# The scan's broadcast loads of the decay sums move from SyncE's queue to GpSimd's

## What is computed

```
a_cs    = cumsum(dt * a_neg)                      # decay sums, per token and head
decay   = exp(where(lower, a_cs[t] - a_cs[s], -inf))
y_diag  = einsum('tsh,shp->thp', cb * decay, xdt)  # cb = C B^T per group
y_off   = einsum('tn,hpn->thp', C, h_in) * exp(a_cs)
y       = y_diag + y_off + d_skip * x
state   = h_in * exp(a_cs[last]) + einsum('sn,shp->hpn', B, xdt * decay_end)
```

## Time and profile before

| | us |
|---|---|
| median of 3 runs | 1619.68 |
| lowest, highest | 1617.15, 1621.8 |
| profiled execution, its own time | 1623.28 |
| its span in the profile | 1621.5 |
| busy: PE, DVE, ACT, POOL | 1359.6, 830.5, 669.1, 265.7 |

### The profile page before, as it was taken

One profiled execution on the slowest core, in us unless ns is written; L12 is line 12 of the kernel. 1 busy time (PEld: TensorE's weight loads), 2 busy tenths in 40 slices (PEclk: granted clock), 3 DMA queues, 4 the chain that ended last, 5 costly groups with the idle time before them and its releaser, 6 DMA issues. The chain is left out here.

```text
span 1621.5 us, 20620 instructions
## 1 busy us (share of the span) xinstructions
PE 1359.6 (84%) x7925; PEld 1190.4 (73%) x7925; DVE 830.5 (51%) x953; ACT 669.1 (41%) x1028; POOL 265.7 (16%) x284
## 2 busy tenths in 40 slices
PE   3999989799998999668888826999974499999980
PEld 1789989799997889645656625998772388888860
DVE  2411432277663111026677666332536189999966
ACT  2423321144442222155567536111131277777753
POOL 0600000000000010044579750000005000000002
PEclk9899999999999999877899856999967699999995
DMA  9982121122112332343454341224246499999945
GB/s 387 405 321 78 53 78 53 36 78 79 60 71 94 128 122 80 115 158 114 132 164 163 130 182 69 79 100 156 93 162 238 158 371 397 415 414 412 404 176 207
DMA packets 61639, 289.09 MB, mean 178 GB/s; under 512 B 8171, under 2 KB 12787, under 8 KB 41206
## 3 DMA queue, kind: packets, MB, share of 16 engines
q1 hardware_dynamic: 48566, 242.18, 40.0%
q0 software_dynamic: 12608, 45.62, 7.2%
q10 hardware_dynamic: 384, 0.16, 0.0%
HBM read 239.51 MB, written 48.43 MB: 178 GB/s over the span
## 5 line engine op out<-in xcount | busy, mean ns | idle before, releaser
L212 PE MATMUL banks<-rounded,rounded 128*128 128x320 f32 (+1 forms) x1168 | 366.8, 314 | 20.1 <-DVE rounded L735 6.9
L213 PE MATMUL banks<-rounded,rounded 128*128 128x320 f32 (+1 forms) x1168 | 364.6, 312 | 0.0
L214 PE MATMUL banks<-rounded,rounded 128*128 128x320 f32 (+1 forms) x1168 | 364.5, 312 | 0.0
L212 PEld LDWEIGHTS banks<-rounded,rounded 128*128 128x128 f32 (+1 forms) x1168 | 221.7, 190 | 21.6 <-issue 13.9
L191 DVE TENSOR_TENSOR rounded<-words,rounded 128x2048 fp32r<-128x2048 f32 x52 | 119.2, 2292 | 226.3 <-ACT rounded L183 224.1
L1889 DVE TENSOR_TENSOR rounded<-words,rounded 128x2048 fp32r<-128x2048 f32 x93 | 212.9, 2290 | 32.9 <-ACT rounded L1880 32.1
L213 PEld LDWEIGHTS banks<-rounded,rounded 128*128 128x128 f32 (+1 forms) x1168 | 221.8, 190 | 0.4
L214 PEld LDWEIGHTS banks<-rounded,rounded 128*128 128x128 f32 (+1 forms) x1168 | 221.5, 190 | 0.3
L1880 ACT ACTIVATE rounded<-words 128x2048 fp32r<-128x2048 f32 x96 | 183.6, 1916 | 46.6 <-PE banks L2007 39.2
L183 ACT ACTIVATE rounded<-words 128x2048 fp32r<-128x2048 f32 x52 | 99.2, 1908 | 140.7 <-PE banks L233 62.7
L1185 ACT ACTIVATE words<-words,words 128x128 f32<-128x128 f32 x320 | 97.8, 388 | 75.4 <-DMA words<-decay_sums 75.4
(11 more groups left out here) (270 smaller groups left out, 2034.7 us busy)
## 6 DMA issues: line engine op xcount, KB each, us to landing
words<-in_units SPq DMA_DIRECT2D x52, 1024.0 KB, 4.9
words<-in_wg SPq DMA_DIRECT2D x32, 1024.0 KB, 8.1
words<-in_wu SPq DMA_DIRECT2D x32, 1024.0 KB, 8.6
words<-in_wd SPq DMA_DIRECT2D x32, 1024.0 KB, 9.4
words<-decay_sums SPq DMA_DIRECT2D x40, 512.0 KB, 3.7
words<-in_w_mod_rest SPq DMA_DIRECT2D x32, 512.0 KB, 5.0
slot_rows<-words POOLq DMA_DIRECT2D x27, 512.0 KB, 21.6
expert_rows<-words POOLq DMA_DIRECT2D x25, 512.0 KB, 9.6
```

Of the source, the lines that this page charges most:

```text
L212: nc.tensor.matmul(out, lhs[0](k), rhs[0](k), start=(k == 0), stop=False)
L213: nc.tensor.matmul(out, lhs[0](k), rhs[1](k), start=False, stop=False)
L214: last = nc.tensor.matmul(out, lhs[1](k), rhs[0](k), start=False, stop=(k == nk - 1))
```

## The change

POOL's program issues the 40 broadcast loads in place of SP's. The first four stand at the head of POOL's program, behind a wait for the stored sums. The others stand in POOL's loop: iteration j, from 1 to 36, issues the load of sub-step j + 3 behind `time_rows(j + 2)` and ahead of `weigh` and `finish_y(j - 1)`. The slots of `E`, the semaphore value that each load waits for and the one that it raises stay as they are. SP keeps the modulation pieces and the stores of the states.

```diff
         @block.sync
-            def spread(j):
-                c, g, q = subs[j]
-                n = (c * 2 * G + 2 * g + q) * 1024
-                if j >= SLOTS:
-                    sp.wait_ge(y_done, j - SLOTS + 1)
-                sp.dma_start(E[:, j % SLOTS, :], scr["sums"][:, n:n + 1024].partition_broadcast(P)).then_inc(sums_spread[j % SLOTS], 16)
...
-            sp.wait_ge(sums_stored, 16 * 16)
-            for j in range(SLOTS):
-                spread(j)
...
             for j in range(NS):
-                if j + SLOTS < NS:
-                    spread(j + SLOTS)
                 if j in at_sub:
                     store_piece(at_sub[j] - 1)
...
         @block.gpsimd
+            def spread(j):
+                c, g, q = subs[j]
+                n = (c * 2 * G + 2 * g + q) * 1024
+                if j >= SLOTS:
+                    pool.wait_ge(y_done, j - SLOTS + 1)
+                pool.dma_start(E[:, j % SLOTS, :], scr["sums"][:, n:n + 1024].partition_broadcast(P)).then_inc(sums_spread[j % SLOTS], 16)
+
+            pool.wait_ge(sums_stored, 16 * 16)
+            for j in range(SLOTS):
+                spread(j)
             pool.wait_ge(scales_done, 2)
...
                 if j + 2 < NS:
                     time_rows(j + 2)
+                if j and j + 3 < NS:
+                    spread(j + 3)
                 for x in x_at[j]:
                     weigh(pool, nc.gpsimd, x)
                 if j > N0:
                     finish_y(j - 1)
```

## The result

The changed kernel takes 1650.94 us (median of four runs, 1649.1 to 1658.53), the kernel before 1619.67 (1617.15 to 1621.8): 1.0203 of it, 95% interval 1.0167 to 1.0238. It is slower by 31.3 us; the forecast was 1620 with a range to 1628. The profiled execution has a span of 1649.9 us, 28.4 more than before. All of that lies in the scan: from the first L1273 to the last it was 220.6 us (710.95 to 931.59) and is 249.0 (710.60 to 959.60).

What follows compares the result with a forecast made beforehand. The scan was taken as bound by a loop of DVE's L1273, PE's products, state product and modulation row, with GpSimd filling up. Terms +0.7 - 1.6 - 0.8 + 1.1 + 0.5 = -0.1 us gave 1620 us, range 1613 to 1628.

Steps and rivals of the forecast that it cites:

- SyncE: 0, loads later: 0.: Removing 40 issues from SyncE gains 0; loads issued later in the scan still leave 2.5 us of room, cost 0.
- second rival: Scan loads from GpSimd land too late, so DVE waits for ACT at L1273: 1623.5 to 1625.5 us; slower-side chance 0.06.
- The price of an issue, 0.54: Each load issue on GpSimd takes 0.54 us, like its direct stores; 22 us more GpSimd work in all.
- first rival: Each GpSimd issue costs 1.29 us, like its indirect ones: about +7.4 us, 1627 us; chance 0.13.
- the third: Rival: DVE's products hold up the issue too, delaying weigh or finish_y: +3.2, 1623 us; counted within the likeliest 0.60.
- The start, +0.7: Four issues ahead of GpSimd's first weigh make it end at 692.9, and the first sub-step follows: +0.7 us.
- Step (b): Issue delays GpSimd's weigh, so L1273 goes first: -1.6 us at iterations 10, 22, 24; -0.8 at 4 and 6.
- (a): Issue hidden under a wait GpSimd has anyway, at iterations 12 to 20 (even), 25 to 29 and 31: 0.
- (d): Issue plainly in the way at iteration 30, where weigh ran alone and PE took it up at once: +0.5 us.
- Step (c): Issue pushes later GpSimd products into DVE's way at iterations 15, 17, 19, 21: +0.28 each, +1.1 us.
- fourth rival: GpSimd's and DVE's products fall in a favourable order, with fewer L1273 waits: -5.2 us, 1614.5 us; chance 0.08.
- The clock: Rival: shifted rhythm moves four PE sub-steps between clock levels, 6.7 us either way: 1613 (chance 0.07) or 1626 us (0.06).

## Why the prediction was wrong, by its own steps

*What bounds the kernel.* The loop that I named holds: DVE's product, PE's products, the state product, the modulation row. That GpSimd "fills up" led me to look for its delays there; it mattered as an obstacle in front of L1273, not as a full engine.

*SyncE: 0, loads later: 0.* Right. The late loads from SyncE cost nothing (0.9995), and the second rival is out: landing takes 4.2 us and at most 6.5, not the 8.8 and 10.3 of the earlier trace rows.

*The price of an issue, 0.54.* Right: 0.578 at the median, 0.597 at most. The first rival (1.29 us) is out, and so is the third, by which DVE's products hold up an issue: none of the 40 took over 0.597, and the one at 848.04 took 0.58 with L1273 running from 847.76 to 849.18.

*The start, +0.7.* The first weigh began at 692.51 and took 1.05 us, so it ended at 693.56, not 692.9, and yet the first L1273 came at 710.60 against 710.95: the term is about 0.

*Step (b), -2.4: this is the step that failed.* It reads "It lets DVE in first", from the rule that "whoever comes first goes first". The rule holds for GpSimd products that have no issue before them. Behind an issue GpSimd's products mostly go before an L1273 that came after the issue's start, until GpSimd pauses: in iterations 10, 22 and 24 L1273 took 3.03 us where it took 1.74, and in 4 and 6 2.48 where it took 1.88. Each term has the opposite sign, +1.3 and +0.6. *Steps (a) and (d)* fall with it: iterations 26, 28 and 30, set down as 0, 0 and +0.5, took 3.03 too. *Step (c)* named sub-steps where a shift of 0.1 us decides; iterations 15 and 17 went from 1.31 to 1.22 and to 1.55, while 13 and 21 went to 1.90. Its size can't be told apart from the rest. The *fourth rival* had L1273's total fall below 57.0; it rose to 69.3.

*The clock* was a rival with no direction, four sub-steps of 1.67 us. Its direction followed from (b): a late L1273 is a longer pause of PE, and the pauses of 2.4 us from 870 on were followed by products at the lower of the two clocks, 3.65 us for 1.97. Its size, by the rough split above, was some 17 us, more than the 6.7 that I had left for it and more than the 12.3 by which L1273 grew.

**Why the products close up** isn't shown. One reading fits: the Trainium skill (Perfetto Trace Analysis, "GPSIMD Engine Instruction" and "DMA Instruction — SWDGE (GPSIMD)") says that GpSimd is eight processors, each with a queue of its own and not synchronized with the others except within an instruction, and that two of them write the descriptors of a DMA. The other six would go on to the weigh while the two are at the issue, and from then on, at every border between two products, one part or the other would still be in a product, until a pause brings them together. The three runs with a memset or a wait agree with it, and so do the L1273 that came at the very start of an issue and got in; the trace doesn't show the processors. Some rows also speak of borders that did open: in the kernel with the issue last, the skip product behind an issue took 1.15 us (L1029 at 791.82) where it takes 0.61, and a DVE product with two SBUF operands, L1210, which had begun at 791.39, in the issue, was through at 792.50, ahead of it. There, too, L1273 came 0.28 us after the start of an issue at 930.53 and at 941.77 and got in ahead of the skip product (1.53 us each). The reading allows that where the product behind the issue is about as long as the issue (0.58); it wasn't tried by itself. It doesn't say why in that kernel the next border, ahead of weigh, let L1273 in at 808.86 (1.92 us) and kept it out at 793.13 (3.60), 1.91 us after the issue's start in both.

## What to carry to other kernels

Price a DMA issue on GpSimd by what stands behind it, not by its 0.58 us: count the products that follow it before GpSimd next truly waits, and ask which two-operand VectorE product arrives after the issue's start and before that wait, and whether TensorE waits for that one. If an issue must stand there, put a wait that outlasts it behind it, or the issue ahead of a wait that can't have been met yet; check that in the trace, since both places where I expected GpSimd to pause anyway were wrong. And where TensorE goes between two clocks, a delay ahead of it is multiplied: try first whether filling its pauses gives the time back (here 0.9915 of the kernel before, from three products in every second sub-step).

## What the runs showed that I had not expected

Delays of 9.4 us in all on VectorE, in six sub-steps, cost 19 to 22 us, and 4.6 with TensorE's pauses filled. Extra products on TensorE, 32 us of them, made the changed kernel 29 us faster. Behind an issue of GpSimd VectorE's product of 1.2 us was kept out for up to 3.1 us more, and for 2.4 where it arrived 1.3 us after the issue had ended; where it came before the issue or with its start it ran as ever.
